# Differential attention without outputs at the meta positions, its rotation by transfers, and layer norm sums of partial sums

## The chip, the cores and the metric

The kernel runs on one core of one Trainium2 chip. It is one program that goes through three blocks of a network. The metric is the time of one execution on the device in microseconds, the median of the runs. Engines are named PE or TensorE (matmul), ACT or ScalarE, DVE or VectorE, POOL or GpSimd, and SP, which issues most loads.

## The reference, cut to what matters

Each of the three blocks takes 512 tokens of width 1024. The first block puts 16 learned meta tokens in front, so that it computes with 528 positions, and cuts them off at its end. Its layer has two mixers side by side, a recurrence over chunks (RWKV) and differential attention, then gates and an output projection, then an MLP with a squared ReLU:

```
x = concatenate([meta_tokens, x])            # 16 + 512 positions
h = rms_norm(x)
y = rwkv(h)                                  # 8 pairs of heads, chunks
for head in 8:                               # differential attention, width 128 = 2 x 64
    q, k = rope(h Wq), rope(h Wk); v = h Wv  # rope turns channels 0..15 of each 64
    a = softmax(q1 k1) - lambda softmax(q2 k2)     # causal
    o = rms_norm(a v) * subln
x = x + (gates * (y Wo, o Wo')) W_out
x = x + relu(rms_norm(x) W1)^2 W2
return rms_norm(x)[16:]
```

The outputs of the differential attention at the 16 meta positions are used by nothing: what follows the mixers takes the 512 positions behind them. Its keys and values at the meta positions are used by all later queries. The rope takes for channels j and j + 8 of each half (j under 8) x cos plus the other channel times sin, once with a minus. The second block begins with a layer norm of its input (ln0) and has one in its middle (ln1); each needs the sum over the 1024 channels of the values and of their squares.

## The kernel before, in words

Channels lie on the 128 partitions and tokens along the free axis, in 8 tiles of 128 x 528 or 128 x 512. Projections are made in three products of high and low parts (`mm3`, line 524), in the rounded type fp32r. Weights come in slabs of 128 x 1024 (512 KB) or in halves of them through a ring of 5 slots; GpSimd splits a half slab into its parts (`pool_half`, line 656: one cast, one subtraction). Matmuls on plain float32 tiles, such as the sum over partitions by a matrix of ones (`colsum`, line 513), are recorded as two rows each.

**The heads stage** (`pe_rwkv`, line 964, and its partners for ScalarE and VectorE) is the loop over 8 pairs of RWKV heads, a chain of small dependent matmuls. Each engine runs the same loop in its own order and waits on semaphores. Two kinds of other work are put between its steps: `work`, the preparation of the next pair and the finish of the last, and `beside`, the differential attention, a generator for each engine (`pe_diff` line 1606, `act_diff` line 1705, `dve_diff` line 1772) that yields 30 times per head. `advance` (line 344) is called at 41 places per pair. Tables written out by hand tell how many steps of either kind are taken there:

```
n = self.place % len(WORK)
work, beside = int(WORK[n]), int(BESIDE[n])
```

LEAD (line 393) is how many steps of the attention are taken with the first preparation. On each engine the order is the program's, so an instruction that waits holds up everything behind it.

**Differential attention, one head.** TensorE projects q, k and v over 528 positions (`lin`, line 1609), in two halves of 264 columns. ScalarE copies q or k out of PSUM (line 1744). VectorE multiplies it with cos (line 1812). TensorE multiplies it with a matrix `rot` that swaps and negates channels (line 1680), VectorE multiplies that with sin out of PSUM and adds (lines 1815 and 1816). Then come five blocks of queries (TK, line 1592): the 16 meta positions, and four blocks of 128. Each has scores with a mask added by a matmul, exponentials on ScalarE, weights on VectorE, transposes of the weights, copies out of PSUM, and the product with V. Square, column sum, root and product make the norm; GpSimd's queue stores the result to DRAM (line 1841).

**Sums over the channels.** `pe_sum8` (line 786) sums squares in 8 accumulating matmuls by ones; for the MLP's norm it stands at line 2007, behind the MLP's second slab. For ln0 the sums of the squares and of the values are made in the last part of the MLP (lines 2019 to 2029), two matmuls for each finished tile. For ln1 `pe_add` (line 732) adds each tile of h to the mean, one matmul behind each of the last slabs of the branches (line 3138). In all three GpSimd has little to do.

**The mixers of the second block** (line 2276) weave three generators in the order of the letters of ORDER (line 2267).

## Time and profile before

| | |
|---|---|
| median of 3 runs | 3085.76 us (3073.72 to 3088.74) |
| the profiled execution | 3070.59 us, its span 3068.7 us |
| granted clock of TensorE, mean | 0.952 |
| busy share of TensorE, VectorE, ScalarE, GpSimd | 92%, 52%, 40%, 28% |
| stages, us from the start of the span | heads to about 966, gates to 1110, MLP to 1521, layer norm to 1560, mixers to 2189, branches to 2338, experts to 2660, third block to 3069 |

A row of the profile is one group of instructions or one stretch of time. The granted clock is the share of TensorE's 2.4 GHz that it got: at any time it is 1.0 or 0.5 (1.2 GHz), and a stretch shows the mean. Matmuls overlap, so the time that a row of one takes is longer than the distance between two starts.

### The profile page before, as it was taken

The numbers are of one execution on the slowest core, as the hardware profiler recorded it, in microseconds if no ns is written. First come the engines' busy times: TensorE is split into PE (matmuls) and PEld (weight loads), VectorE is DVE, ScalarE is ACT, GpSimd is POOL, SyncE is SP. The second block draws the span as 40 slices with busy tenths as digits, with TensorE's granted clock in tenths as the row PEclk, the third lists the DMA queues.
The fourth block names the chain that finished last, engine by engine and source line by source line (L and its number), as shares of the span: only waits on it lengthen the run. The fifth ranks groups of instructions, "written<-read, shape, count | busy, mean of one in ns | idle before, by whom it ended". The sixth has DMA issues, their size and how long they took to land.

```text
span 3068.7 us, 53994 instructions
## 1 busy us (share of the span) xinstructions
PE 2826.4 (92%) x22582; PEld 2275.8 (74%) x22582; DVE 1601.6 (52%) x2907; ACT 1215.1 (40%) x2134; POOL 849.2 (28%) x849
## 2 busy tenths in 40 slices
PE   7899999989998999999989988998897999899997
PEld 7788888878876877887667777776775888566565
DVE  4545644555432544343244446456666899844553
ACT  2423433342331233233242434353325777534341
POOL 5222222212224200000143535353100027454233
PEclk9989998999899999999998999999999999899999
DMA  4111111111114332333121212221433888421122
GB/s 140 36 33 42 34 40 36 39 29 40 39 51 172 117 110 89 96 95 91 51 66 52 80 51 77 63 76 55 158 100 123 327 318 335 167 76 56 42 59 69
DMA packets 104003, 286.24 MB, mean 93 GB/s; under 512 B 11696, under 2 KB 11824, under 8 KB 102480
## 3 DMA queue, kind: packets, MB, share of 16 engines
q1 hardware_dynamic: 83408, 209.11, 22.2%
q0 software_dynamic: 15024, 62.14, 5.5%
q10 hardware_dynamic: 5328, 11.54, 1.0%
q8 instruction: 179, 2.93, 0.4%
q14 instruction: 64, 0.52, 0.1%
HBM read 262.81 MB, written 19.92 MB: 92 GB/s over the span
## 4 chain that ended last, share of the span: by engine, by line
PE 70%; DVE 17%; ACT 9%; issue 2%; DMA 2%; ACTq 0%; DVEq 0%; SPq 0%; POOLq 0%
PE psum L497 68%; DVE arena L429 9%; ACT arena L414 4%; ACT arena L422 3%; DVE arena L438 3%; PE psum L501 2%; ACT L409 1%; DVE ring L429 1%; DMA ring<-in_w 1%; DVE arena L433 1%; DVE arena L441 1%; DVE arena L453 0%; DVE arena L450 0%; DMA arena<-in_x 0%; DVE arena L457 0%
## 5 line engine op out<-in xcount | busy, mean ns | idle before, releaser
L497 PE MATMUL psum<-arena,ring 128*128 128x512 f32 (+3 forms) x6280 | 1453.9, 365 | 16.9 <-DVE arena L429 6.0
L497 PEld LDWEIGHTS psum<-arena,ring 128*128 128x128 f32 (+2 forms) x6280 | 1047.3, 193 | 210.9 <-issue 36.8
L497 PE MATMUL psum<-arena 32*32 32x32 f32 (+18 forms) x12332 | 798.8, 244 | 138.2 <-DVE arena L429 46.1
L497 PE MATMUL psum<-arena,arena 128*128 128x512 f32 (+2 forms) x3004 | 844.3, 386 | 37.0 <-DVE arena L429 15.1
L497 PEld LDWEIGHTS psum<-arena 32*32 32x32 f32 (+10 forms) x12332 | 581.4, 136 | 322.1 <-issue 113.4
L497 PEld LDWEIGHTS psum<-arena,arena 128*128 128x128 f32 x3004 | 541.4, 189 | 171.4 <-issue 25.2
L441 POOL CAST ring<-ring 128x512 fp32r<-128x512 f32 x348 | 234.6, 674 | 1357.1 <-DMA ring<-in_w 1213.5
L422 ACT ACTIVATE arena<-psum 128x512 f32<-128x512 f32 (+12 forms) x682 | 295.3, 450 | 752.0 <-PE psum L497 598.4
L429 DVE TENSOR_TENSOR arena<-arena 128x256 f32<-128x256 f32 (+8 forms) x681 | 361.8, 544 | 229.7 <-ACT arena L414 115.9
L429 POOL TENSOR_TENSOR ring<-ring,ring 128x512 fp32r<-128x512 f32 x348 | 465.8, 1338 | 28.0
L414 ACT ACTIVATE arena<-arena 128x512 f32<-128x512 f32 (+10 forms) x532 | 305.2, 583 | 343.0 <-DVE arena L429 160.9
L422 ACT ACTIVATE arena<-ring 128x1024 fp32r<-128x1024 f32 (+1 forms) x180 | 180.7, 1004 | 391.5 <-PE psum L497 324.4
L429 DVE TENSOR_TENSOR ring<-ring,arena 128x1024 fp32r<-128x1024 f32 (+1 forms) x180 | 207.7, 1154 | 199.8 <-ACT arena L422 196.1
L429 DVE TENSOR_TENSOR arena<-arena,psum 88x192 f32<-88x192 f32 (+4 forms) x276 | 111.9, 419 | 304.6 <-PE psum L497 301.1
L438 DVE SCALAR_TENSOR_TENSOR arena<-arena 128x512 f32<-128x512 f32 (+8 forms) x244 | 171.4, 703 | 181.0 <-ACT arena L414 175.1
L422 ACT ACTIVATE arena<-arena 128x1024 fp32r<-128x1024 f32 (+5 forms) x274 | 191.7, 706 | 67.8 <-DVE arena L429 27.0
L429 DVE TENSOR_TENSOR arena<-arena,arena 128x1024 fp32r<-128x1024 f32 (+5 forms) x198 | 206.8, 1044 | 19.0 <-ACT arena L422 12.1
L414 ACT ACTIVATE arena<-psum,arena 128x528 f32<-128x528 f32 (+7 forms) x174 | 99.5, 579 | 166.6 <-PE psum L497 96.6
L501 PE MATMUL psum<-arena 128*128 128x128 f32 (+3 forms) x749 | 119.4, 291 | 42.7 <-DVE arena L429 12.9
L429 DVE TENSOR_TENSOR arena<-psum,arena 88x264 f32<-88x264 f32 (+7 forms) x209 | 94.5, 490 | 87.9 <-PE psum L497 50.3
L501 PEld LDWEIGHTS psum<-arena 128*128 128x128 f32 (+3 forms) x749 | 89.7, 141 | 67.5 <-DVE arena L429 14.1
L438 DVE SCALAR_TENSOR_TENSOR arena<-psum,arena 128x512 f32<-128x512 f32 (+2 forms) x89 | 54.8, 628 | 150.6 <-PE psum L497 134.9
(52 smaller groups left out, 843.6 us busy)
## 6 DMA issues: line engine op xcount, KB each, us to landing
ring<-in_w SPq DMA_DIRECT2D x372, 256.0 KB, 2.7
ring<-in_w SPq DMA_DIRECT2D x133, 512.0 KB, 3.5
arena<-in_w SPq DMA_DIRECT2D x61, 512.0 KB, 5.5
bg<-arena ACTq DMA_DIRECT2D x24, 256.0 KB, 2.2
yd<-arena ACTq DMA_DIRECT2D x7, 512.0 KB, 7.2
arena<-bg POOLq DMA_DIRECT2D x1, 3072.0 KB, 16.8
arena<-in_x SPq DMA_DIRECT2D x1, 2112.0 KB, 8.1
od<-arena POOLq DMA_DIRECT2D x8, 256.0 KB, 2.3
```

Source lines behind the costliest of these rows:

```text
L409: self.eng.preload_act_table_set(name)
L414: self.own(self.ready().activation(out, a, f, bias=bias, scale=scale, accum_out=accum), event)
L422: self.own(self.ready().activation(out, a, ACT.Copy, scale=scale), event)
L429: self.own(self.ready().tensor_tensor(out, a, b, op), event)
L433: self.own(self.ready().tensor_scalar(out, a, s1, None, op0), event)
L438: self.own(self.ready().scalar_tensor_tensor(out=out, in0=a, scalar=s, in1=b, op0=op0, op1=op1), event)
L441: self.own(self.ready().tensor_copy(out, a), event)
L497: self.last_ins = self.eng.matmul(out, l, r, start=start, stop=stop, skip_group_check=skip)
L501: self.last_ins = self.eng.transpose(out, a, self.ident[0:n, 0:n])
```

## The change

1. Differential attention makes q, scores, weights and outputs for 512 positions only; k and V keep all 528. TK has four blocks, a head has 27 steps. The first product of the values contracts over 128 rows, of which 112 are zero (set once).
2. The matrix `rot` and its matmuls go. ScalarE issues, behind its copy, four transfers of 8 partitions that write the swapped rows into a tile `rot` (the fourth tile of weights, used later in the head); VectorE multiplies that tile with a sine table that holds the signs and is zero elsewhere. ScalarE waits for the rope before it overwrites the tile.
3. GpSimd adds the tiles 0 to 6 of three kinds of sums, and TensorE sums that tile and tile 7: for the MLP's norm, for ln0 (squares and values) and for the mean of ln1. (For ln1 the sum of squares stays.) In the mixers GpSimd waits for the mean of ln0 as well.
4. New tables: WORK, BESIDE (its digits sum to 216, and to 240 before), LEAD 8 in place of 9, and ORDER, which has the same letters in slightly another order.

```diff
-            sin[h + j] = sin[h + 8 + j] = np.sin(ang[:, j])
-            rot[h + 8 + j, h + j] = -1.0
-            rot[h + j, h + 8 + j] = 1.0
+            sin[h + 8 + j] = np.sin(ang[:, j])
+            sin[h + j] = -sin[h + 8 + j]
...
-    "11044040000111120112121000121103120100000"
+    "00020051021420102201311101010001013100010"
...
-LEAD = 9
+LEAD = 8
...
+    d.rot = d.P[3]
...
-TK = [(0, 16)] + [(16 + 128 * j, 128) for j in range(4)]
+TK = [(META + 128 * j, 128) for j in range(4)]
...
 def pe_diff(K, m):
...
+                if n == 2:
+                    pe_terms(K, m, b, wh(k), wl(k), kx)
+                else:
+                    P.mm3([ps[:, 512 * b:512 * b + tokens]], wh(k), wl(k), m.hx_r[kx], m.lx_r[kx], kx == 0, kx == 7)
...
-        P.mm(o, d.V[0:16, 0:128], d.am[0:16, 128 * (i % 2):128 * (i % 2) + qw], True, i == 0)
+        P.mm(o, d.V[:, 0:128], d.am[:, 128 * (i % 2):128 * (i % 2) + 128], True, False)
...
-            yield from lin(3 * hd + i, ("df_qk", nme, hd))
-            yield
-            P.colsum(("df_rot", nme, hd), ("df_sin", nme, hd), c["rot"], [d.q if nme == "q" else d.k], T, [("df_qk", nme, hd)])
+            yield from lin(3 * hd + i, ("df_qk", nme, hd), T2 if nme == "q" else T)
+            yield
...
-        P.colsum(("df_sum", hd), ("df_root", hd), c["ones"], [d.t2], T, [("df_osq", hd)])
+        P.colsum(("df_sum", hd), ("df_root", hd), c["ones"], [d.t2[:, 0:T2]], T2, [("df_osq", hd)])
...
+def swapped(x):
+
+    return [x[h + r:h + r + 8] for h in (0, 64) for r in (0, 8)]
...
 def act_diff(K, m):
...
+            if hd or i:
+                A.wait_ge(*(at("df_roped", "q", hd) if i else at("df_roped", "k", hd - 1)))
+            n = x.shape[1]
+            for r, (to, of) in enumerate(zip(swapped(d.rot), (1, 0, 3, 2))):
+                A.ready().dma_start(to[:, 0:n], swapped(x)[of]).then_inc(*K.book.up("df_rot", ("df_rot", nme, hd, r), by=16))
             yield
...
 def dve_diff(K, m):
...
-            V.apart().wait_ge(*at("df_rot", nme, hd))
-            V.apart().tt(h2(d.t2), out_of(K, 2, T, "df_sin", nme, hd), h2(c["sin"]), MUL, "df_sin", nme, hd)
-            V.tt(x, d.t1, d.t2, ADD, "df_roped", nme, hd)
+            V.apart().tt(d.t1[:, 0:n], x, c["cos"][:, o:T], MUL)
+            yield
+            V.apart().wait_ge(*at("df_rot", nme, hd, 3))
+            V.apart().tt(d.t2[:, 0:n], d.rot[:, 0:n], c["sin"][:, o:T], MUL)
+            V.tt(x, d.t1[:, 0:n], d.t2[:, 0:n], ADD, "df_roped", nme, hd)
...
 def pool_gates(K, m, gk):
...
+    for k in range(1, 7):
+        if k == 1:
+            G.wait_ge(*at("sq", "mlp", 0))
+        G.wait_ge(*at("sq", "mlp", k))
+        G.tt(m.odh[:, 0:T], m.odh[:, 0:T], m.odh[:, k * T:k * T + T], ADD, "mg_sq", k)
+    for k in range(1, 7):
+        S = slice(k * T, k * T + T)
+        if k == 1:
+            G.wait_ge(*at("xsq", 0))
+        G.wait_ge(*at("xsq", k))
+        G.tt(m.sqx[:, 0:T], m.sqx[:, 0:T], m.sqx[:, S], ADD)
+        G.tt(m.acc_out, m.out[:, 0:T] if k == 1 else m.acc_out, m.out[:, S], ADD, "mg_x", k)
...
 def pe_mlp(K, m):
...
-                pe_sum8(K, "mlp", m.odh, T)
+                P.colsum(("sum", "mlp"), ("root", "mlp"), K.c["ones"], [m.odh[:, 0:T], m.odh[:, 7 * T:8 * T]], T, [("mg_sq", 6), ("sq", "mlp", 7)])
...
+    P.wait_ge(*at("mg_x", 6))
+    P.mm(K.ps[:, 512 * bs:512 * bs + 512], K.c["ones"], m.sqx[:, 0:T], True, False)
+    P.mm(K.ps[:, 512 * bm:512 * bm + 512], K.c["ones"], m.acc_out, True, False)
+    P.wait_ge(*at("xsq", 7))
+    P.mm(K.ps[:, 512 * bs:512 * bs + 512], K.c["ones"], m.sqx[:, 7 * T:8 * T], False, True)
+    P.mm(K.ps[:, 512 * bm:512 * bm + 512], K.c["ones"], m.out[:, 7 * T:8 * T], False, True)
...
 def pool_mixers(K, m):
...
+    G.wait_ge(*at("mean", "ln0"))
...
 def pe_branches(K, m):
...
+    K.P.colsum(("mean", "ln1"), ("centred", "ln1", 7), K.c["ones"], [m.h_acc, m.h[:, 7 * T2:8 * T2]], T2, [("b_hacc", 6), ("b_h", 7)])
...
 def pool_branches(K, m, bg):
...
+    for k in range(1, 7):
+        if k == 1:
+            G.wait_ge(*at("b_h", 0))
+        G.wait_ge(*at("b_h", k))
+        G.tt(m.h_acc, m.h[:, 0:T] if k == 1 else m.h_acc, m.h[:, k * T:k * T + T], ADD, "b_hacc", k)
```

## Rows read from the trace of the kernel before

**Rows 1.** The page, part 1: busy time of each engine.

```profile
PE 2826.4 (92%) x22582; PEld 2275.8 (74%) x22582; DVE 1601.6 (52%) x2907; ACT 1215.1 (40%) x2134; POOL 849.2 (28%) x849
```

**Rows 2.** Busy time by stage: heads, a stretch of the MLP, mixers.

```profile
core 0: us, PE busy (x) PEld busy (x) DVE busy (x) ACT busy (x) POOL busy (x), PEclk, DMA share, GB/s
...
59.00:966.00 907.00, 844.39 (x12324) 729.95 (x12323) 443.28 (x1077) 314.46 (x756) 237.00 (x246) 0.93 0.14 41
1200.00:1300.00 100.00, 100.00 (x434) 81.31 (x433) 36.55 (x39) 28.30 (x34) 0.00 (x0) 1.00 0.32 95
...
1560.00:2189.00 629.00, 571.54 (x3953) 462.87 (x3953) 322.60 (x565) 257.52 (x415) 264.96 (x260) 0.94 0.23 66
```

**Rows 3.** The chain of waits in the heads stage, 59 to 966 us, by line.

```profile
by line: PE psum L497 73.3%; DVE arena L429 8.6%; ACT arena L422 4.1%; PE psum L501 4.1%; ACT arena L414 3.1%; issue 2.4%; DVE arena L438 1.1%; ACT L409 0.8%; DVE arena L453 0.8%; DVE arena L457 0.7%; DVE arena L433 0.3%; DVE arena L450 0.3
```

**Rows 4.** Groups of TensorE instructions by form, heads stage.

```profile
line engine op names shapes xcount | busy us, mean ns | idle before us <-releasers
L497 PE MATMUL psum<-arena,ring 128*128 128x264 f32 x2196 | 319.3, 300 | 6.2 <-issue 5.1 <-ACT arena L422 0.7 <-DVE arena L429 0.4
...
L497 PE MATMUL psum<-arena 128*128 128x264 f32 x256 | 74.8, 418 | 4.9 <-ACT arena L414 3.3 <-DVE arena L429 1.3 <-ACT arena L422 0.3
L497 PE MATMUL psum<-arena,ring 128*128 128x512 f32 x272 | 70.2, 412 | 0.3 <-ACT arena L422 0.3
...
L497 PE MATMUL psum<-arena 128*128 128x128 f32 x160 | 31.6, 339 | 0.0
...
L497 PE MATMUL psum<-arena 16*128 16x128 f32 x64 | 17.4, 355 | 6.7 <-ACT arena L422 6.7
...
L497 PE MATMUL psum<-arena 16*128 16x16 f32 x16 | 3.4, 284 | 3.1 <-ACT arena L422 3.1
L497 PE MATMUL psum<-arena 64*16 64x16 f32 x32 | 1.7, 180 | 0.0
L497 PE MATMUL psum<-arena_halved 16*16 16x16 bf16 x16 | 1.6, 168 | 0.0
L501 PE MATMUL psum<-arena 16*16 16x16 f32 x8 | 1.4, 178 | 1.3 <-DVE arena L438 1.3
```

**Rows 5.** TensorE in order of time, two projections at full clock.

```profile
start us, us, engine line op out<-in xcount [idle before <-releaser]
...
59.44 12.06 PE L497 MATMUL psum<-arena,ring 128*128 128x264 f32 x96
71.33 0.83 PE L497 MATMUL psum<-arena 128*128 128x264 f32 x3
```

**Rows 6.** In order of time, one rope: copy, then product with the sine.

```profile
181.58 0.61 ACT L422 ACTIVATE arena<-psum 128x528 f32<-128x528 f32 x1 [9.02 <-PE psum L497]
...
183.66 0.71 DVE L429 TENSOR_TENSOR arena<-psum,arena 128x528 f32<-128x528 f32 x1 [0.41 <-PE psum L497]
```

**Rows 7.** Transfers issued by ScalarE: the 24 of L2617, landing; the 6 of gk.

```profile
L2617 ACTq DMA_DIRECT2D bg<-arena x24: 326/326/327, 1643.5 to 2187.1; - x24
...
DMA to landing us min/median/max: 2.0/2.2/3.6
...
gk<-arena ACTq DMA_DIRECT2D x6, 256.0 KB, 2.8
```

**Rows 8.** TensorE in order of time, last part of the MLP, one k.

```profile
1439.18 1.88 PE L497 MATMUL psum<-arena 128*128 128x512 f32 x4
...
1452.00 1.88 PE L497 MATMUL psum<-arena 128*128 128x512 f32 x4
```

**Rows 9.** TensorE in order of time, end of the branches, one k.

```profile
2278.78 1.02 PE L497 MATMUL psum<-arena 128*128 128x512 f32 x2
...
2285.17 1.02 PE L497 MATMUL psum<-arena 128*128 128x512 f32 x2
```

**Rows 10.** GpSimd in order of time: a two-input operation beside VectorE, and alone.

```profile
1062.13 2.27 POOL L429 TENSOR_TENSOR arena<-arena,arena 128x512 fp32r<-128x512 f32 x1 [3.25 <-DVE arena L441]
...
1095.41 1.30 POOL L429 TENSOR_TENSOR arena<-arena,arena 128x512 fp32r<-128x512 f32 x1 [14.45 <-DVE arena L441]
```

More of the change, by code:

```diff
@@ L52, in constants @@
     cos, sin = np.ones((128, T1)), np.zeros((128, T1))
-    rot = np.zeros((128, 128))
     for h in (0, 64):
@@ L1607, in pe_diff, with lin @@
     P, at, ps, c, T, d = K.P, K.book.at, K.ps, K.c, T1, m.df
-    def lin(i, emptied):
-        b = P.bank(2, *emptied)
-        P.keep(b, 2)
+    def lin(i, emptied, tokens):
+        n = 2 if tokens > 512 else 1
+        b = P.bank(n, *emptied)
+        P.keep(b, n)
         for half in range(2):
@@ L1638, in scores @@
             for q, k, meta, rest, most in half:
-                P.mm(meta, c["ident16"][0:16, 0:16], c["negm16"][0:16, 0:16], False, True)
+                P.mm(rest[:, 0:W - 144], q, k[:, 16:W - 128])
         else:
-            if nb == 2:
-                for q, k, meta, rest, most in half:
-                    P.mm(meta, q, k[:, 0:16])
-                for q, k, meta, rest, most in half:
-                    P.mm(rest[:, 0:W - 144], q, k[:, 16:W - 128])
-            else:
-                for q, k, meta, rest, most in half:
-                    P.mm(most, q, k[:, 0:W - 128])
@@ L1649, in scores @@
-            for q, k, meta, rest, most in half:
-                P.mm(rest[:, W - 144:W - 16], q, k[:, W - 128:W], True, False)
-            for q, k, meta, rest, most in half:
-                P.mm(rest[:, W - 144:W - 16], c["ident16"][:], c["negm16"][:], False, True)
+            for q, k, meta, rest, most in half:
+                P.mm(most, q, k[:, 0:W - 128])
+        for q, k, meta, rest, most in half:
+            P.mm(rest[:, W - 144:W - 16], q, k[:, W - 128:W], True, False)
+        for q, k, meta, rest, most in half:
+            P.mm(rest[:, W - 144:W - 16], c["ident16"][:], c["negm16"][:], False, True)
@@ L1653, in scores @@
         P.did("df_score", hd, i)
     def values(hd, i):
[L1656 to L1657 removed]
+        aw = d.P[2 * (i % 2)]
         P.wait_ge(*at("df_w", hd, i))
[L1659 to L1664 removed]
+        b = P.bank(2 if i == 3 else 1, "df_wt", hd, i)
@@ L1665, in values @@
+        m0, n0 = weights_at(b, i)
+        P.tr(ps[0:META, m0:m0 + 128], aw[:, 0:META])
+        for j in range(i + 1):
+            P.tr(ps[:, n0 + 128 * j:n0 + 128 * j + 128], aw[:, TK[j][0]:TK[j][0] + 128])
         P.did("df_tr", hd, i)
@@ L1690, in pe_diff @@
         behind = None
-        for i in range(5):
+        for i in range(4):
             scores(hd, i)
@@ L1756, in act_diff @@
         behind = None
-        for i in range(5):
+        for i in range(4):
             scores(hd, i)
@@ L1775, in scores @@
     def scores(hd, i):
-        q0, qw = TK[i]
-        W = q0 + qw
+        W = TK[i][0] + 128
         nb = 2 if W > 512 else 1
-        sc = [d.sc[0:qw, 6 * i + 3 * sub:6 * i + 3 * sub + 3] for sub in range(2)]
-        Pt = [d.P[2 * (i % 2) + sub][0:qw, 0:W] for sub in range(2)]
+        sc = [d.sc[:, 6 * i + 3 * sub:6 * i + 3 * sub + 3] for sub in range(2)]
+        Pt = [d.P[2 * (i % 2) + sub][:, 0:W] for sub in range(2)]
         for sub in range(2):
```

155 lines of the change are left out of this document (67 added, 88 removed).

## The prediction

> **What bounds the kernel now.** I read the page first: TensorE is busy for 92% of the span, every other engine for about half of it or less [rows 1]. The reader should see one engine that is almost never free. Then I cut the span into stages [rows 2]. The heads stage (the row 59:966) has 844 us of matmuls in 907 us at a granted clock of 0.93, so 63 us without a matmul and some 14% of the stage at the lower clock level (0.93 = 1 - 0.14/2). The stretch 1200:1300, inside the MLP, has no idle time and full clock: 434 matmuls in 100 us, 0.230 us each. The mixers have 571.5 of 629 us. So whatever leaves TensorE in the MLP is worth its full length; what leaves it in the heads stage is worth its length less what the other engines cannot follow. The chain of that stage says how much that is: 77% is on TensorE, about 12% on VectorE and 8% on ScalarE, 2% issue [rows 3].
>
> **The change part by part, heads stage.** All of this is TensorE work of the differential attention, 8 heads.
> - *The rotation matmuls go.* Two per head (q and k), each over two halves, each half recorded as two rows: 64 of the 256 rows of the 128x264 form, 74.8 us together, 0.292 each [rows 4]: 18.7 us. Rows overlap a little, so this is the upper end. From below: a full-precision matmul over 512 columns costs 0.88 us (worked out below), over 264 columns 0.45, and there are 32: 14.5 us. I take 16.5.
> - *q for 512 positions and not 528.* 24 pairs of 264-column matmuls per head become 24 single ones of 512. By the busy time of the two forms, 319.3/2196 = 0.145 and 70.2/272 = 0.258 [rows 4]: 2 x 0.145 - 0.258 = 0.033 us, times 192 = 6.3 us. At full clock the halves take (71.33 - 59.44)/96 = 0.124 [rows 5], against 0.230: 0.018 each, 3.3 us. I take 5.
> - *The block of 16 meta queries goes:* its scores (32 rows and 16 mask rows), its transposes (8) and its values (16 rows): 1.7 + 1.6 + 1.4 + 3.4 = 8.1 us busy, and 3.1 + 1.3 us of idle time in front of them [rows 4]. Between 8.1 and 12.5; I take 10.
> - *The column sum of the output norm* goes from 32 rows of 264 columns (9.3 us at 0.292) to 8 matmuls of 512 (7.0 us at 0.88). The columns alone say 3%, 0.3 us; I take 1, with 2.3 as the other end.
> - *The first values matmul* now contracts over 128 rows, of which 112 are zeros, and no longer over 16. Columns are the same. The 16-row form takes 17.4/64 = 0.272, the 128-row form 31.6/160 = 0.198 [rows 4]. So up to 4.7 us of gain; a loss has no row that speaks for it. The 16-row ones stand behind waits, which explains the difference without the rows, so I take nothing.
>
> Sum: 32.5 us off TensorE, between 26 and 44.5.
>
> *What comes instead.* The rotation is done by four transfers of 8 partitions per q and per k, 64 in all, issued by ScalarE. Now the sine product starts 183.66 - (181.58 + 0.61) = 1.47 us after the copy out of PSUM ends [rows 6]. A transfer issued by ScalarE holds it 0.326 us and lands 2.2 us (median, in the heads stage 2.8) after its issue [rows 7]. The fourth is issued three issues after the copy, 0.98 us, and lands at 3.2 to 3.8 us: the sine product is 1.7 to 2.3 us later, 16 times, 27 to 37 us of VectorE, with everything of the other mixer that stands behind it in VectorE's order: masks, inverses, state updates. ScalarE is held 4 x 0.326 = 1.3 us, 16 times, 21 us; behind it stand the copies out of PSUM that TensorE's banks wait for. Its own new waits (rotation of k after q is roped) end long before, since a whole projection lies between. These are transfers within SBUF, and the rows are stores to HBM. The Trainium skill (DMA: Bandwidth & Descriptors, Anatomy of one DMA) puts a fixed 2.0 us on every transfer, mostly the write receipt, heaviest for HBM; by that the landing would be 0.2 us earlier and 16 x 0.2 = 3 us of VectorE's time would come back; no row here has such a transfer. How much of 37 + 21 = 58 us reaches TensorE? Nothing, if the new step tables leave a gap between the two steps; all of it, if they never do. VectorE and ScalarE hold 20% of the chain [rows 3], so I take 20%: 11 us back. The transfers' data, 64 x 17 KB, is nothing.
>
> *The new tables WORK, BESIDE and LEAD* follow from the 27 steps per head that were 30. What they are worth beyond that no row shows. They can only win or lose idle time, of which there are 63 us; I take 0 and keep 10 to either side. Net for the heads: 32.5 - 11 = 21.5 us.
>
> **MLP and branches.** A full-precision matmul of 512 columns: from 1439.18 to 1452.00 there are 48 ordinary ones and 2 of these, 12.82 - 48 x 0.2304 = 1.76, 0.88 each [rows 8]. In the branches: 2285.17 - 2278.78 - 24 x 0.2304 = 0.86 [rows 9].
> - The sum of squares of the MLP's norm: 8 become 2, 6 x 0.88 = 5.3 us.
> - The two sums for the layer norm behind the MLP: 16 become 4, 12 x 0.88 = 10.6 us. Four stood behind the last slab before and four do after, so the tail stays.
> - The mean of ln1: 8 become 2, 6 x 0.86 = 5.2 us.
>
> Sum 21.1 us. The cover: GpSimd makes 24 additions of 128x512. A two-input operation of that size takes 1.30 us on it, and 2.27 beside a busy VectorE [rows 10]. One k of the MLP's last part is 12.8 us of TensorE and brings two additions, at most 4.5 us, one k of ln1 is 6.4 us and brings one. So the sixth partial sum is ready before the last slab ends. If the cover went, each of the three sums would wait for one addition, 2.3 us, 7 in all. Behind the additions stand on GpSimd's queue the first four half slabs of the mixers (each one such operation and a cast), which TensorE wants only after the layer norm and, after ln1, only the slot table. The 2.27 speaks against GpSimd: the Trainium skill (SBUF — State Buffer, Who interferes with whom) says that a GpSimd operation reading SBUF and a VectorE one with two SBUF inputs lock each other out for a whole instruction. By it 24 x 1.3 = 31 us of VectorE could be blocked, and the sum stands only because VectorE has that slack: it is busy for 36.6 of 100 us in the MLP stretch [rows 2].
>
> *ORDER* differs in a few places; the counts of the letters are the same. Nothing, 5 us to either side of the 57 us without matmuls [rows 2].
>
> **The sum:** 21.5 + 21.1 = 42.6 us. The profiled execution took 3070.6 us, so 3028; it is 15 us below the median of the runs, 3085.8, and below the lowest, 3073.7. Against the median: 3043 us, 1.4% less.
>
> **Rivals.**
> 1. *The tables win more.* TensorE's idle time in the heads falls by a third, 21 us, or the transfers are wholly hidden (11): about 3022. For it: 63 us of it are there [rows 2], and all three tables are new. Against: filler goes away, which leaves less to put in the gaps.
> 2. *The heads give everything back.* The stage is bound by the recurrence of the other mixer, and the removed matmuls were filler beside its waits; only the 21 us of the MLP and branches stay: 3065. The change then doesn't do what it says for the meta positions. For it: 23% of the chain is off TensorE. Against: 93% of the stage has a matmul running.
> 3. *The clock.* What goes is dense work of wide matmuls; what stays has 3648 matmuls of 32x32. If the granted clock of the heads fell from 0.93 to 0.90, 0.06 x 880 = 53 us more would run at 1.2 GHz in place of 2.4, and cost about half, 26 us: 3069. The Trainium skill (TensorE: Matmul & The Clock Gate, What's actually happening) has the throttled state as the default, which only activity releases.
> 4. *Slower: each rope stalls the recurrence.* In VectorE's order the state update stands right behind the sine product, so TensorE stands for 2.3 + 1.3 us, and the stall drops the clock: 3.6 us and some 2 us more at the lower level, 16 times 5.6 = 90 us against 53.6 saved: 3122. It makes the kernel slower from 53.6/16 = 3.4 us per rope on, and by more than 0.5% from (53.6 + 15)/16 = 4.3. Against: both halves would have to be fully on the path each time.
>
> **How the numbers follow.** The forecast has 0.57, the rivals 0.20, 0.11, 0.08 and 0.04. The range goes from the upper ends of the terms with some of rival 1 (44.5 + 21.1 + 12 off 3085.8: 3008) up to rivals 2 and 3 with a few us of scatter, 3072. A measurement here can tell about 0.5% (15 us; the three runs spread as much). Faster by more, below 3070: forecast, rival 1, most of 2, half of 3: 0.87. Within: 0.09. Slower: 0.04.
>
> **What would show it.** Right: 64 + 32 rows fewer of the 264-column full-precision form (of 256), 64 transfers of ScalarE; in the heads stage some 30 us less TensorE busy time and the stage 15 to 30 us shorter; the wait of VectorE's sine product on a transfer near 2 us, 16 times; 28 full-precision rows of 512 columns and not 64 from the MLP to the layer norm behind it, a stretch 16 us shorter with no new idle time; no TensorE wait on GpSimd in front of the sums. Wrong: a heads stage as long as before with more than 63 us without matmuls (rivals 2, 4), its clock below 0.91 (3), or a TensorE wait for GpSimd of over 2 us.

## The result, and the profile after

The changed kernel takes 2966.4 us (median of 4 runs, 2960.4 to 2975.3) against 3085.2 before: 0.962 of the time, with a 95% interval of 0.959 to 0.966. I had forecast 3043 with a range of 3008 to 3072. The sign was right, the size was not: 119 us came off and not 43, and the result lies below the whole range. In the profiled executions it is 3070.6 to 2964.7, 105.9 us. The profile of before is one of its faster executions (the median is 3085), that of after is near its median.

The page of after, part 1:

```profile
PE 2754.9 (93%) x22190; PEld 2211.0 (75%) x22190; DVE 1615.9 (55%) x2854; ACT 1207.8 (41%) x2086; POOL 883.2 (30%) x873
```

TensorE is still the bound; 71.5 us less of it are busy [rows 1]. The other 34 of the 106 us were time without a matmul. Where both went is read by cutting both traces at the same work (to within 0.7 us). Busy time by stage, before: heads, gates, MLP, mixers, branches, the rest (columns as in [rows 2], whose first row ends inside the last head).

```profile
59.00:989.40 930.40, 859.61 (x12389) 742.00 (x12387) 448.21 (x1083) 319.43 (x762) 243.39 (x254) 0.93 0.16 48
989.40:1108.00 118.60, 113.93 (x481) 91.06 (x481) 59.71 (x71) 29.26 (x35) 29.70 (x21) 0.97 0.41 134
1108.00:1533.90 425.90, 419.12 (x1745) 329.46 (x1746) 158.79 (x178) 139.25 (x180) 10.47 (x12) 0.99 0.28 84
...
1533.90:2189.70 655.80, 591.19 (x4032) 476.33 (x4033) 340.47 (x602) 271.32 (x435) 277.15 (x273) 0.93 0.23 66
2189.70:2338.10 148.40, 131.92 (x512) 97.73 (x511) 88.03 (x121) 50.36 (x73) 6.19 (x8) 0.96 0.39 128
2338.10:3068.70 730.60, 667.42 (x3144) 499.78 (x3144) 480.34 (x806) 385.61 (x620) 255.80 (x252) 0.96 0.47 162
```

The same stages after:

```profile
59.00:926.70 867.70, 804.28 (x12065) 688.39 (x12063) 446.81 (x1027) 311.76 (x714) 240.17 (x254) 0.96 0.18 52
926.70:1044.60 117.90, 114.61 (x481) 91.42 (x481) 59.75 (x71) 29.25 (x35) 29.67 (x21) 0.98 0.40 132
1044.60:1455.40 410.80, 404.02 (x1709) 322.20 (x1710) 160.65 (x178) 139.33 (x180) 35.42 (x30) 0.99 0.30 89
...
1455.40:2091.30 635.90, 592.99 (x4030) 472.81 (x4030) 347.03 (x601) 271.52 (x435) 278.19 (x273) 0.94 0.23 68
2091.30:2234.90 143.60, 128.56 (x501) 97.60 (x502) 92.75 (x123) 50.36 (x73) 16.54 (x14) 0.94 0.40 133
2234.90:2962.90 728.00, 667.21 (x3144) 500.12 (x3143) 481.01 (x806) 385.65 (x620) 256.23 (x252) 0.96 0.47 162
```

Row against row: heads -62.7, gates -0.7, MLP -15.1, mixers -19.9, branches -4.8, the rest -2.6; together 105.8. Three readings follow.

**MLP and branches are the forecast** (15.9 and 5.2), with no new idle time.

**The mixers lose 19.9 us and no busy time** (591.2, then 593.0; 4032 and 4030 rows). Two things differ there: ORDER, and that GpSimd waits for the mean of ln0.

**The heads lose 55.3 us of busy time and 7.4 of idle time.** The granted clock goes from 0.93 to 0.96: at the lower level (1.2 GHz) the stage spent about 2 x 0.07 x 930 = 130 us before and 2 x 0.04 x 868 = 69 after. Work there takes twice as long, so 61 us less of it is worth some 30. Then 55.3 - 30 = 25 us of matmuls really went. (The clock column has two digits, so each of the two products is good to about 9 us. Cut into stretches of 5 us, in which the clock is nearly always 1.0 or 0.5, and added up, the same column gives 125 us before and 67 after, with 26 us of matmuls gone. Times at the lower level further down are read in this finer way.)

TensorE by form in the heads stage, after:

```profile
L495 PE MATMUL psum<-arena,ring 128*128 128x264 f32 x1856 | 258.5, 293 | 1.8 <-issue 1.1 <-ACT arena L420 0.7
...
L495 PE MATMUL psum<-arena 128*128 128x264 f32 x160 | 43.8, 397 | 5.5 <-ACT arena L420 1.6 <-ACT arena L412 1.5 <-DVE arena L427 1.3
L495 PE MATMUL psum<-arena 128*128 128x128 f32 x224 | 38.1, 317 | 3.8 <-ACT arena L420 2.3 <-issue 1.4
...
L499 PE MATMUL psum<-arena 128*88 128x128 f32 x192 | 26.7, 278 | 12.0 <-DVE arena L427 12.0
...
L495 PE MATMUL psum<-arena 128*128 128x512 f32 x16 | 9.0, 644 | 0.1
```

As forecast, 96 of the 256 full-precision rows of 264 columns are gone, and the forms with 16 query columns are gone with them. The values products stood in two rows before, 31.6 for 160 and 17.4 for the 64 with 16 rows [rows 4]. Now they are one form, 224 for 38.1: 10.9 us less for the same columns. A part of that is bookkeeping: neighbouring matmuls overlap, and a group that is split in two counts the overlap in both (all forms of this stage add up to 957 us where TensorE is busy for 804).

Who VectorE waits for in the heads stage, after, and then the 64 transfers as ScalarE issues them (the first starts just before the stage's cut, so the view has 63):

```profile
DVE arena L427 <- DMA arena<-arena: 42.9, 14, 5.1
```

```profile
L1753 ACTq DMA_DIRECT2D arena<-arena x63: 631/632/1320, 58.9 to 778.7; - x63
```

The wait that I had foreseen is there, 42.9 us in 14 waits, 3.1 each. An issue holds ScalarE 0.63 us, not the 0.33 of [rows 7], 2.65 us for a set of four. One rope in order of time, ScalarE and then VectorE:

```profile
171.87 0.60 ACT L420 ACTIVATE arena<-psum 128x512 f32<-128x512 f32 x1 [9.57 <-PE psum L495]
172.50 2.65 ACTq L1753 DMA_DIRECT2D arena<-arena  x4
175.20 1.30 ACT L420 ACTIVATE arena<-psum 128x528 f32<-128x528 f32 x2 [2.73 <-issue]
...
176.62 1.42 DVE L427 TENSOR_TENSOR arena<-arena 128x512 f32<-128x512 f32 x2 [3.43 <-DMA arena<-arena]
```

In the view 172.47 is where the copy ends (171.87 + 0.60). The sine product starts 176.62 - 172.47 = 4.15 us after it; before it was 1.47 [rows 6]. And the stage got shorter all the same.

### The profile page after: what moved, and what is told of

Read it like the earlier page. It is cut to its first block, busy times and chain, and to the rows that moved or that the text cites. A ratio compares the mean times of both kernels' runs of the same rounds, so it can differ in the third digit from the quotient of the medians.

```text
span 2962.9 us, 53223 instructions
## 1 busy us (share of the span) xinstructions
PE 2754.9 (93%) x22190; PEld 2211.0 (75%) x22190; DVE 1615.9 (55%) x2854; ACT 1207.8 (41%) x2086; POOL 883.2 (30%) x873
## 3 DMA queue, kind: packets, MB, share of 16 engines
q1 hardware_dynamic: 83408, 209.04, 22.8%
## 4 chain that ended last, share of the span: by engine, by line
PE 68%; DVE 18%; ACT 8%; issue 2%; DMA 2%; ACTq 1%; POOL 0%; DVEq 0%; SPq 0%; POOLq 0%
PE psum L495 66%; DVE arena L427 10%; ACT arena L412 4%; DVE arena L436 3%; ACT arena L420 3%; PE psum L499 2%; DVE ring L427 2%; DMA ring<-in_w 1%; ACT L407 1%; DVE arena L431 1%; DVE arena L439 1%; ACTq L1753 1%; DVE arena L451 0%; DVE arena L458 0%; DVE arena L448 0%
## 5 line engine op out<-in xcount | busy, mean ns | idle before, releaser
L495 PE MATMUL psum<-arena,ring 128*128 128x512 f32 (+2 forms) x6088 | 1440.2, 369 | 12.6 <-DVE arena L427 5.7
L495 PEld LDWEIGHTS psum<-arena,ring 128*128 128x128 f32 (+1 forms) x6088 | 1021.7, 191 | 217.4 <-issue 40.0
L495 PE MATMUL psum<-arena 32*32 32x32 f32 (+16 forms) x12156 | 738.4, 240 | 118.5 <-ACT arena L412 36.9
L495 PEld LDWEIGHTS psum<-arena 32*32 32x32 f32 (+10 forms) x12156 | 542.5, 134 | 290.7 <-issue 114.9
L420 ACT ACTIVATE arena<-psum 128x512 f32<-128x512 f32 (+15 forms) x666 | 292.5, 456 | 694.6 <-PE psum L495 564.7
L420 ACT ACTIVATE arena<-arena 128x1024 fp32r<-128x1024 f32 (+5 forms) x274 | 191.8, 707 | 66.3 <-DVE arena L427 25.6
L412 ACT ACTIVATE arena<-psum,arena 128x512 f32<-128x512 f32 (+7 forms) x158 | 95.3, 611 | 147.9 <-PE psum L495 84.4
L427 POOL TENSOR_TENSOR arena<-arena 128x512 f32<-128x512 f32 x24 | 35.3, 1472 | 400.8 <-ACT arena L412 371.5
L499 PE MATMUL psum<-arena 128*128 128x128 f32 (+2 forms) x741 | 118.4, 291 | 35.7 <-DVE arena L427 17.9
L427 DVE TENSOR_TENSOR arena<-psum,arena 88x264 f32<-88x264 f32 (+6 forms) x193 | 83.3, 472 | 97.9 <-PE psum L495 53.6
L499 PEld LDWEIGHTS psum<-arena 128*128 128x128 f32 (+2 forms) x741 | 89.3, 142 | 59.5 <-DVE arena L427 19.8
```

Source lines behind the costliest of these rows:

```text
L412: self.own(self.ready().activation(out, a, f, bias=bias, scale=scale, accum_out=accum), event)
L420: self.own(self.ready().activation(out, a, ACT.Copy, scale=scale), event)
L427: self.own(self.ready().tensor_tensor(out, a, b, op), event)
L495: self.last_ins = self.eng.matmul(out, l, r, start=start, stop=stop, skip_group_check=skip)
L499: self.last_ins = self.eng.transpose(out, a, self.ident[0:n, 0:n])
```

## The experiments

What the trace left open: why the clock of the heads rose, what the tables are worth, whether the transfers cost anything, and whether ORDER alone explains the mixers. The theories were: the removed TensorE work itself (the forecast's way); the 112 zero rows of the first values matmul, if they keep the clock up; the new tables; the new ORDER. Every expectation was written before its run. All ratios are to the kernel before on the same chip, with the 95% interval. Stages are cut as above; where only a stage's length is given, it is read from the same view.

How far a stage moves by itself is seen in kernels whose code is the same there. The heads take 930.4, 931.9 and 939.1 us in the three profiles with before's heads (before, experiments 1 and 5), and 867.7, 867.1, 859.3 and 861.4 in the four with after's. So a difference of under 9 us between two profiles shows nothing. The three with before's heads have 125, 132 and 152 us at the lower level: what moves is the clock.

**1. ORDER alone, from both sides.** After with the old string:

```diff
-    "dddddlldldddlldddlldlldllldlldldddlddgldddldgdldgllggldgldglgldldllddllddldlldldldlddldldddddllldlldl"
+    "ddddddddldddldddllldldllldldlllldldgdddlddlgdldglldldglgdgggllldldldldldlldlddldldddlddldddlddlddlll"
...
```

> The kernel after with the ORDER of before. The heads stage became 62 us shorter, the mixers 19 us (655 to 636) with 23 us less time without a matmul. Theory A (the new ORDER made the mixers' gain): the mixers go back to some 655 us and the total is 15 to 20 us longer than after. Rival B (the mixers gained because GpSimd now waits for the mean of ln0 and the PSUM banks are handed out from another start, and the order of letters is nothing): the mixers stay near 636 and the total within 5 us of after.

Measured: 2990.0 us, ratio 0.970 (0.967 to 0.974). The mixers of this kernel:

```profile
1449.50:2108.50 659.00, 592.45 (x4032) 475.87 (x4033) 344.45 (x603) 271.33 (x435) 276.48 (x273) 0.93 0.22 65
```

659.0 against 635.9, the 655.8 of before again, with the busy time unchanged. The other side, before with the new string:

> The kernel before with the new ORDER alone. Undone in the kernel after, ORDER made the mixers 23 us longer (27 us more time without a matmul). Theory A (a better order of the same work, whatever else is changed): the mixers 18 to 25 us shorter than the 656 to 665 of before, the total 0.6 to 0.8% less. Rival B (it fits only the kernel after, where GpSimd waits and the banks start elsewhere): less than 8 us.

Measured: 3049.2 us, ratio 0.991 (0.989 to 0.994), and the mixers are as short as in after:

```profile
1533.00:2168.30 635.30, 592.63 (x4030) 472.62 (x4030) 344.47 (x601) 271.57 (x435) 280.52 (x273) 0.94 0.22 68
```

GpSimd's wait is not in this kernel, so ORDER does it alone. It is worth 20.5 to 23 us in the profiles (both cuts with the old string stand 0.7 us late, so 20 to 22), whatever stands around it. Over all runs of this document the mixers take 655 to 664 us with the old string (five profiles) and 627 to 643 with the new one (thirteen). Which waits it takes away is seen in who TensorE waits for in the mixers, before:

```profile
PE psum L497 <- DVE arena L429: 25.0, 21, 3.7
PE psum L497 <- DVE arena L438: 12.0, 2, 7.1
...
PE psum L501 <- DVE arena L438: 6.5, 2, 5.5
PE psum L501 <- ACT arena L422: 4.6, 1, 4.6
```

and before with the new ORDER:

```profile
PE psum L497 <- DVE arena L429: 12.9, 14, 2.3
...
PE psum L497 <- DVE arena L438: 7.0, 3, 4.8
...
PE psum L501 <- DVE arena L438: 1.1, 2, 0.7
PE psum L501 <- ACT arena L422: 0.8, 2, 0.5
```

These four go from 48.1 to 21.8 us; others rise a little, and all idle time of the stage goes from 64.6 to 42.7. The counts of the letters are the same, but 192 of the 380 places hold another letter. That the places where TensorE caught up with VectorE now have other work in them is my reading of these rows.

**2. The zero rows.** After, with only the 16 rows that hold meta values multiplied (32 matmuls, recorded as 64 rows of the profile):

```diff
-        P.mm(o, d.V[:, 0:128], d.am[:, 128 * (i % 2):128 * (i % 2) + 128], True, False)
+        P.mm(o, d.V[0:META, 0:128], d.am[0:META, 128 * (i % 2):128 * (i % 2) + 128], True, False)
```

> The kernel after, but the first product of the values contracts over the 16 rows that hold numbers and not over 128 rows with 112 of zeros. Theory A (zero rows keep the granted clock up): half of the clock's gain in the heads goes, 10 to 20 us longer than after, clock 0.94. Rival B (the rows are nothing, only columns count): within 5 us, the form of 16 rows at the 0.27 us that it had before against 0.17 for 128 rows, at most 6 us longer.

Measured: 2993.2 us, ratio 0.971 (0.967 to 0.974). The heads:

```profile
59.00:955.30 896.30, 838.55 (x12067) 714.30 (x12066) 445.15 (x1028) 311.57 (x714) 240.95 (x254) 0.92 0.17 51
```

28.6 us longer: 34.3 us more busy time and 5.7 us less idle time (57.8 against 63.4), with 138 us at the lower level and not 67. So the clock didn't fall for want of work: from 140 to 158 us TensorE is busy without a gap in this trace, and the clock falls at about 151, while after has the full clock through the same steps. Leaving out a product by zeros that costs no columns makes the kernel slower. The opposite edit, before with all 128 rows and the zeros they need:

```diff
-        P.mm(o, d.V[0:16, 0:128], d.am[0:16, 128 * (i % 2):128 * (i % 2) + qw], True, i == 0)
+        P.mm(o, d.V[:, 0:128], d.am[:, 128 * (i % 2):128 * (i % 2) + qw], True, i == 0)
...
+    V.apart().ms(d.am, 0.0)
+    V.apart().ms(d.V[:, 0:128], 0.0, "df_zero")
```

> The kernel before, with the first product of the values over 128 rows (112 of zeros) and no longer over 16; nothing else. In the kernel after, the reverse edit made the heads stage 29 us longer, all by the clock (138 and not 67 us at the lower level, idle time 6 us less). Theory A (zero rows keep the clock up by themselves): the heads stage 15 to 30 us shorter than before, 60 to 80 us at the lower level where 125 were. Rival B (it works only with the new tables): within 5 us of before.

Measured: 3045.9 us, ratio 0.990 (0.987 to 0.993). The heads:

```profile
59.00:964.60 905.60, 831.09 (x12389) 721.74 (x12388) 449.31 (x1084) 318.85 (x762) 243.40 (x254) 0.96 0.16 49
```

930.4 becomes 905.6, and 0.93 becomes 0.96 (70 us at the lower level for 125), with the same 12389 rows and idle time that even grows by 3.7. The whole time falls by 1.0% (0.7 to 1.3). In the kernel before the edit also widens the product of the meta block, which after doesn't have. About a quarter of what the change gains (24.8 of 105.9 us) is this one slice. Half way, after with 64 rows (`d.V[0:64, ...]`, `d.am[0:64, ...]`):

> The kernel after with the first product of the values over 64 rows (48 of zeros): between the 16 rows (heads stage 896 us, 138 us at the lower clock) and the 128 rows (868 and 867 us, 67 and 69 us). Theory A (the clock follows how many rows matmuls use, by degrees): heads stage 875 to 890 us, 85 to 115 us at the lower level. Rival B (only a full array counts): 892 to 900 us and 125 us or more. Rival C (anything more than 16 rows does): 865 to 870.

Measured: 2989.7 us, ratio 0.971 (0.967 to 0.976), and the heads:

```profile
59.00:948.50 889.50, 829.08 (x12068) 705.20 (x12067) 444.05 (x1028) 311.49 (x714) 242.29 (x254) 0.94 0.17 51
```

16, 64 and 128 rows give 896, 890 and 868 us at 0.92, 0.94 and 0.96, with 138, 110 and 67 us at the lower level. The step from 64 to 128 rows is clear. That from 16 to 64 isn't resolved: 6.8 us is within the scatter, and the whole kernel has the ratio 0.971 both times. The Trainium skill (TensorE: Matmul & The Clock Gate, What's actually happening) says that the clock is set by how busy TensorE has been lately. These runs add what counts as busy: instructions of the same length and number, over fewer rows of the array, hold the clock less.

**3. The tables.** After with WORK, BESIDE and LEAD of before as they stand (240 steps for 216):

> The kernel after with WORK, BESIDE and LEAD of before, whose digits hand out 240 steps where 216 are left, so that each head of the attention moves forward against the pair it was beside. Theory A (the new step tables made what the heads stage gained beyond the removed matmuls, by raising the granted clock from 0.93 to 0.96): the heads stage is 25 to 40 us longer than after, with a clock of 0.93 or less. Rival B (the removed work itself did it, through the clock): within 10 us of after, clock 0.95 or more.

Measured: 3076.6 us (10 runs), ratio 1.001 (0.998 to 1.004); the heads take 983.2 us, 115 more than after, at a clock of 0.89 and with 122.8 us idle. Each head of the attention now moves forward against the pair that it was beside, so this says that the tables must fit the steps, not what the re-cut is worth. For that I cut the digits of the three steps per head that no longer exist out of BESIDE of before, and kept WORK and LEAD of before:

```diff
-    "12000000020211110010102210201210010101021"
+    "12000000010101110010102210201210010101021"
...
```

> The kernel after with WORK and LEAD of before and BESIDE of before from which only the 24 steps of the meta block are taken out (of each head steps 13, 14 and 16), so that every other step of the attention stays at its place beside the pairs. It asks what the new tables are worth when the old ones are not thrown out of step: with the old digits as they stood the heads stage was 115 us longer, with 207 us at the lower clock. Theory A (the tables kept the attention in step, and that is all they had to do): within 10 us of after. Theory B (the search over the tables is itself worth a good part of the heads' gain, by clock and by idle time): heads stage 15 to 40 us longer than after, more idle time than 63 us and more than 90 us at the lower clock.

Measured: 3007.6 us, ratio 0.978 (0.974 to 0.982). The heads:

```profile
59.00:963.20 904.20, 815.15 (x12067) 695.81 (x12066) 441.06 (x1028) 312.54 (x714) 239.43 (x254) 0.96 0.17 51
```

36.5 us longer than after, 25.6 of them idle time (89.0 against 63.4); 81 us are at the lower level, 67 in after. Who TensorE waits for there:

```profile
PE psum L495 <- DVE arena L427: 30.0, 33, 2.4
PE psum L495 <- ACT arena L420: 16.4, 21, 2.9
```

and in after:

```profile
PE psum L495 <- DVE arena L427: 19.3, 23, 7.6
...
PE psum L495 <- ACT arena L420: 7.3, 14, 1.2
```

**4. Transfers against rotation matmuls.** After with the rotation matrix and its matmuls back, and the transfers out:

```diff
+            P.colsum(("df_rot", nme, hd), ("df_sin", nme, hd), c["rot"], [d.q if nme == "q" else d.k], T2 if nme == "q" else T, [("df_qk", nme, hd)])
...
-            for r, (to, of) in enumerate(zip(swapped(d.rot), (1, 0, 3, 2))):
-                A.ready().dma_start(to[:, 0:n], swapped(x)[of]).then_inc(*K.book.up("df_rot", ("df_rot", nme, hd, r), by=16))
```

> The kernel after with the rotation by matmuls again and no transfers. Theory A (the transfers are worth the matmuls they replace): 16 to 19 us longer. Rival B (the 43 us for which VectorE waits for the landings, and ScalarE's issues, reach TensorE in part): 0 to 10 us longer. Rival C (the dense matmuls kept the clock up): shorter or the same, with less time at the lower level.

Measured: 2973.3 us, ratio 0.966 (0.963 to 0.970), and the heads:

```profile
59.00:931.40 872.40, 815.03 (x12115) 693.75 (x12113) 444.65 (x1027) 311.94 (x714) 242.53 (x254) 0.97 0.17 51
```

Against after the stage is 4.7 us longer: 10.7 us more matmul time and 6.0 less idle time. That is within the scatter, and the runs as a whole (2973 and 2966) don't tell them apart beyond their intervals. The same edit with the trimmed tables of experiment 3:

> The kernel after with the trimmed tables (those of before without the 24 steps of the meta block) and with the rotation by matmuls: beside before_128_rows this leaves the removed meta outputs alone, in the heads. With the transfers the trimmed tables gave 904 us, 1 us less than before with 128 rows, though 27 us of matmuls were gone. Theory A (the transfers need the new tables: with the old places VectorE and ScalarE hold up the chain and the clock falls): 15 to 25 us shorter than the trimmed kernel with transfers, 880 to 890 us of heads. Rival B (the old places do not suit heads of 27 steps either way): within 8 us of it.

Measured: 3005.3 us, ratio 0.977 (0.973 to 0.981), and the heads:

```profile
59.00:962.50 903.50, 823.05 (x12118) 699.75 (x12116) 444.76 (x1028) 312.95 (x714) 243.04 (x254) 0.96 0.16 50
```

903.5 against 904.2 with transfers: nothing either way, rival B. And the transfers alone, in before with its own tables:

```diff
-            P.colsum(("df_rot", nme, hd), ("df_sin", nme, hd), c["rot"], [d.q if nme == "q" else d.k], T, [("df_qk", nme, hd)])
...
+            for r, (to, of) in enumerate(zip(swapped(d.rot), (1, 0, 3, 2))):
+                A.ready().dma_start(to[:, 0:n], swapped(x)[of]).then_inc(*K.book.up("df_rot", ("df_rot", nme, hd, r), by=16))
```

> The kernel before with the rotation by transfers, its tables unchanged. VectorE's step that waits for the landing stands in these tables mostly one place behind the step before it. Theory A (the landings are hidden even so): 14 to 19 us shorter than before. Rival B (they are hidden by the new tables only): VectorE waits about 2 us 16 times, and the heads stage is 0 to 8 us shorter, or longer.

Measured: 3086.5 us (10 runs), ratio 1.003 (1.000 to 1.006). The heads of this run:

```profile
59.00:1012.20 953.20, 876.50 (x12325) 757.69 (x12323) 447.09 (x1084) 318.96 (x762) 240.93 (x254) 0.90 0.16 48
```

The 64 rotation rows are gone (12389 - 12325) and the busy time is 17 us higher, at a clock of 0.90: 199 us at the lower level for 125. But this profile is too dark a picture. It took 3095.6 us, 9 above the median of its own runs, while that of before lies some 15 below its median; by the ratio the kernel is 0.3% slower (0.0 to 0.6), and not 0.8% as by the two profiles. So the forecast 14 to 19 us didn't come, and a loss is at the edge of what these runs can show. VectorE waits for the landings no longer than in after:

```profile
DVE arena L427 <- DMA arena<-arena: 45.1, 15, 3.8
```

45.1 us here, 42.9 there. So it isn't the length of the wait that sets the two apart, and whether it is its place in the order isn't shown. A lower clock ate what the matmuls freed; that a stall of TensorE at each rope brought it down is not shown either, since idle time is only 5.9 us more (76.7 against 70.8).

**5. GpSimd's sums alone**, in before (the kernel's other parts as they were):

```diff
-                pe_sum8(K, "mlp", m.odh, T)
+                P.colsum(("sum", "mlp"), ("root", "mlp"), K.c["ones"], [m.odh[:, 0:T], m.odh[:, 7 * T:8 * T]], T, [("mg_sq", 6), ("sq", "mlp", 7)])
...
+        G.tt(m.acc_out, m.out[:, 0:T] if k == 1 else m.acc_out, m.out[:, S], ADD, "mg_x", k)
```

> The kernel before with GpSimd's partial sums alone (for the MLP's norm, ln0 and the mean of ln1; the wait for the mean of ln0 in the mixers with them). By the prediction's sum: 21 us less than before, 16 of them in the MLP and 5 in the branches, no wait of TensorE for GpSimd over 1 us; heads stage unchanged. Rival (the sums also move the mixers, through other PSUM banks and GpSimd's wait): the mixers change by more than 8 us, so that the total is 10 or 35 us less.

Measured: 3054.4 us, ratio 0.990 (0.985 to 0.995): 20.3 us less in the medians, and the forecast 21 us (0.7%) lie inside the interval. The MLP takes 411.0 us against 425.9 before and 410.8 after, so the whole 15 us there is these sums; the branches take 143.1. The mixers take 660.3 and so don't gain from GpSimd's wait. The heads, whose code is that of before, are 8.7 us longer in this profile (the scatter above). GpSimd in order of time in after, the last additions of the MLP:

```profile
1412.38 2.66 POOL L427 TENSOR_TENSOR arena<-arena 128x512 f32<-128x512 f32 x2 [8.50 <-ACT arena L412]
1423.54 2.66 POOL L427 TENSOR_TENSOR arena<-arena 128x512 f32<-128x512 f32 x2 [8.50 <-ACT arena L412]
```

Two additions take 2.66 us of every 11.16 (1423.54 - 1412.38), 1.33 each, so the cover that I named held with room. TensorE waits for GpSimd once in the branches, 0.8 us; before it did so twice, 1.4. From the MLP to the layer norm the full-precision rows of 512 columns go from 68 to 32, the 36 fewer that the forecast had.

**6. Is it additive?** Before with three edits only, all shown above: 128 rows, the new ORDER, the sums. Meta outputs, rotation and tables stay.

> The kernel before with the zero rows, the new ORDER and GpSimd's sums, and with its meta outputs, its rotation by matmuls and its own WORK and BESIDE. If the parts add up: heads 905 us, MLP 411, mixers 633 to 636, branches 145: the profile at 3002 us or so (3068.7 - 25 - 15 - 21 - 3), the ratio 0.978. If they share a gain: above 3015.

Measured: 3006.5 us, ratio 0.976 (0.972 to 0.981). Heads 908.6, MLP 410.7, mixers 633.9: each as in its own experiment, within the scatter. These three bring 2.4% of the change's 3.4 to 3.8%. The rest, some 1%, is the removed meta outputs, the transfers and the new tables together, and of these only the tables stand out of the noise: with the trimmed ones and rotation matmuls the ratio is 0.977, with the new ones 0.966.

**7. The clock lever once more.** The recurrence in the heads stage has a product over 32 rows too (the low-rank part of its gate, at the end of each pair). After with 128, the missing ones zero:

```diff
-            P.mm(o, p["g2b"][0:32, 128 * hp:128 * hp + 128], m.lora[2][0:32, J], False, True)
+            P.mm(o, p["g2b"][:, 128 * hp:128 * hp + 128], m.lora[2][:, J], False, True)
...
+    V.apart().ms(m.lora[2], 0.0)
```

> An attempt at a faster one on the same principle as the zero rows: the kernel after, with the gate's second product of the RWKV finish (16 full-precision matmuls, 32 rows of the profile, which contract over 32 partitions) widened to 128 partitions, 96 of them zeros. If time at the lower clock follows how many of the 128 rows matmuls use anywhere in the heads: 5 to 10 us shorter than after, under 60 us at the lower level. If only the values' product stands at a place where it counts: within 3 us.

Measured: 2958.7 us, ratio 0.962 (0.958 to 0.967), beside after itself once more:

> The kernel after, unchanged, on the chip of the three that follow and with as many rounds: 0.962 of before, and the measure of how far the heads stage (868 us) and its time at the lower clock (67 us) move by themselves. All theories expect 855 to 880 us and 50 to 85 us.

Measured: 2965.5 us, ratio 0.964 (0.960 to 0.967). A difference of 6.8 us is too near the noise, so both were timed again, with more runs.

> The kernel after with the gate's product of 32 rows widened to 128, once more with five rounds: its heads stage was 861 us against 868 and 867. If that gain is real, 5 to 8 us (0.2%) below after_five of the same chip; if it was an accident of the one profile, no difference.

> The kernel after on the chip of the three others, five rounds: 0.962 to 0.964 of before, heads stage 865 to 870 us.

Measured: 2963.2 (0.964, 0.960 to 0.968) and 2968.9 us (0.966, 0.962 to 0.969). The medians differ by 5.7 us in the same direction, but the intervals overlap almost wholly, and the stage that the edit is in doesn't show it: the heads take 860.7 and 863.6 us in the two profiles with the edit and 859.3 to 867.7 in the four without. The mixers, which the edit doesn't touch, move more: 642.4 and 626.5 us with it, 635.9, 632.0 and 635.6 in the three profiles of after. This stays open; I claim no version better than after.

## Why the prediction was wrong

**The heads as a ladder.** Each step is one run of the list above, each length a row of the same view:

| kernel | heads, us | idle in it | at the lower level | step |
|---|---|---|---|---|
| before | 930.4 | 70.8 | 125 | |
| before, 128 rows | 905.6 | 74.5 | 70 | zero rows: -24.8 |
| meta outputs gone (q and the norm's sum for 512), trimmed tables, rotation matmuls | 903.5 | 80.5 | 66 | -2.1 |
| new tables, rotation matmuls | 872.4 | 57.4 | 61 | re-cut tables: -31.1 |
| after (transfers) | 867.7 | 63.4 | 67 | -4.7 |

The forecast for these 62.7 us was 21.5. With a scatter of up to 9 us, the steps of -2.1 and -4.7 can't be told from nothing; the other two can, and the ratios of the whole kernel say the same (0.990 for the zero rows, 0.977 to 0.966 for the tables).

**"The first values matmul ... so I take nothing": the first step that failed.** It is worth 24.8 us added to before and 28.6 taken from after. I had the two forms side by side, 0.272 and 0.198 us [rows 4], and explained the difference by waits, though idle time has a column of its own there and is no part of the 17.4 us. I bounded the gain by what the instruction itself could win, 4.7 us; the gain was in the clock under everything that stood around it, 125 us at the lower level to 70. I had this mechanism as rival 3, and with the wrong sign: dense wide work goes, so the clock falls. It rose.

**"The new tables ... I take 0 and keep 10 to either side": the second.** Once the steps are gone, re-cut tables are worth 31.1 to 36.5 us against the plainly trimmed ones; these are one way of trimming, so the figure is for that way. My bound used the 63 us of idle time but allowed a sixth of it. What I missed is on the second rung: without the re-cut, taking the meta outputs away brings 2.1 us, because the 8.0 us of busy time that go (831.1 to 823.1) come back as 6.0 us of waiting. By these two profiles that is rival 2, filler that turns into idle time until the tables are fitted; both differences are within the scatter, but the ratios agree: 0.976 for before with three edits, 0.977 for the kernel with the same three and without the meta outputs. Rival 1, tables that win more, came true: the re-cut takes 23.1 us of idle time (80.5 to 57.4) where it had 21, and 31.1 us in all (8.0 are busy time, though I had written that tables can only win or lose idle time). Idle time from before to after fell only by 7.4, since the removed work had first added to it.

**"ORDER: nothing, 5 us to either side": the third.** It was worth 20.5 to 23 us. "The counts of the letters are the same" was no argument for anything: 57 us without a matmul stood in that stage, and where a letter stands decides how much of them stays. And "differs in a few places" was a wrong reading of the change: 192 of the 380 letters differ.

Added up, these three are 76 to 88 us that the sum had at zero. In the profiles the result was 63 below the forecast and not 76: the removed matmuls and the transfers brought 6.8 us of their 21.5 on the ladder, which hid 15 of it. That 76 is also near the 77 by which the medians missed is chance.

**The removed matmuls: too high.** 32.5 us forecast, 26 the lower end; 26 measured between before and after (55.3 busy less 29 of clock), but the ladder gives only part of that to the removed work. For the rotation matmuls I took 16.5: the pair with trimmed tables shows 7.9 us of busy time (823.1 against 815.2), the pair with new tables 10.7. Both kernels with transfers had more time at the lower level (81 against 66 us, 67 against 61); with half of that added the pairs give 15 and 14 us, my lower end. For the meta outputs, the wider q and the norm's sums I took 16, and on the second rung they took 8.0, or 6 at the same clock. So some 20 of the 26 are the removed work, and the last term is the one that was mis-sized.

**The transfers: the net was near, the parts not.** I had 16.5 gained and 11 given back, 5.5 net; 4.7 in the heads with the new tables, -0.7 with the trimmed ones, both within the scatter, so that the first is so near is luck. VectorE's wait was 42.9 us and not 27 to 37, since an issue takes 0.63 us and not 0.33 and the fourth is issued later. The Trainium skill (DMA: Bandwidth & Descriptors, Anatomy of one DMA) has a fixed 2.0 us per transfer, measured for those that GpSimd issues; here the fourth issue of the rope above ends at 175.15, began some 0.63 earlier, and the product starts at 176.62, 2.1 us after that, which agrees for ScalarE's. Rival 4, the stall that drops the clock, had a lower clock come with the transfers in before's tables only. There the heads are 22.8 us longer in one profile and the kernel 6 us in the medians, far from its 90.

**MLP and branches: right**, 21.1 forecast, 19.9 measured, with the cover on GpSimd as described. The lock between GpSimd and VectorE that the Trainium skill states (SBUF — State Buffer, Who interferes with whom) reached TensorE with nothing: its idle time in the MLP is 6.8 us before and after. VectorE's busy time there is 158.8 and 160.7; no run tells how long either engine was held off.

**The allowance for the profiled execution.** I added 15 us for the medians of before. After's profiled run lies only 1.7 us below its own median, so of the 77 us 13 come from there; in profiles the forecast was 3028 and the result 2964.7, 63 below.

**The range** took the terms one by one and bounded each unknown by a few us around nothing. It left out that three of them could all be large and of one sign.

What stays open: which property of the matmuls the clock follows. The runs show that rows multiplied matter at equal columns and counts, for this stage and this product, and no row shows why; the gate's product over 32 rows showed no such gain. Products of the scores still contract over 64 rows and weren't tried wider. Nor were two transfers for the rotation in place of four.

## What to carry to other kernels

An edit that gives TensorE the same columns and more rows isn't free of effect: in a stage whose granted clock is below 1, read the clock column before and after, and don't slice the zeros off an operand without measuring. A hand-written order of work is a term of the sum like any other: bound it by the idle time of its stage, not by a habit, and expect removed filler to bring little until the order is fitted again. Before crediting a change to the part it is named after, run the parts alone; here two thirds came from three small ones. And before reading a few us out of one profile, look how far stages with the same code lie apart.

## What the runs showed of the hardware

- Zero rows hold TensorE's clock up: 32 full-precision matmuls (64 of the stage's 12,000 rows in the profile), widened from 16 to 128 rows, moved the stage's granted clock from 0.92 to 0.96 and its length from 896 to 868 us. In the kernel before, 0.93 to 0.96 and 930 to 906 us.
- The clock can fall while TensorE is never idle: with 16 rows it fell at about 151 us, in the midst of 18 us without a gap (140 to 158).
- ScalarE needed 0.63 us to issue a transfer of 8 partitions within SBUF, and 0.33 us for the stores of [rows 7].
- With a step order that doesn't fit, more waiting and a lower clock come together: the old tables in after gave 59 us more idle time and a clock of 0.89 for 0.96 (207 us at the lower level for 67), 115 us in all.
